# A router whose dense gate blocks are built earlier and stored in parts: stages swapped, picks moved up, sums of every third batch moved to VectorE

## The chip, the cores and the metric

The kernel runs on one core of a Trainium2 chip. The time is device time in microseconds (us) of one execution, as the median of several runs; lower is better. The engines are PE (TensorE), DVE (VectorE), ACT (ScalarE), POOL (GpSimd) and SP (SyncE), and 16 DMA engines move data between HBM and the on-chip memory. POOL issues the gathers here, SP most other transfers.

## What is computed

One layer of a decoder: attention branches, and then a channel mixer (PEER) with 16384 experts. Only the mixer matters here; it takes more than half of the time.

```
q = (hx @ w_pq).reshape(PEER_BLOCK, PEER_HEADS, 2, PK_HALF)
s = jnp.einsum('nhpc,hpkc->nhpk', q, sub_keys)
top_s, top_i = lax.top_k(s, PEER_TOPK)
cand = top_s[:, :, 0, :, None] + top_s[:, :, 1, None, :]
best_s, best = lax.top_k(cand.reshape(...), PEER_TOPK)
eidx = i1 * N_KEYS + i2
g = jax.nn.softmax(best_s, axis=-1)
a = jax.nn.gelu(jnp.einsum('nd,nhkd->nhk', hx, expert_u[eidx])) * g
return jnp.einsum('nhk,nhkd->nd', a, expert_v[eidx])
```

There are 1032 tokens (1024 and 8), 1024 features, 8 heads with two sets of 128 keys, and the 16 best pairs of each head: 128 experts for each token.

## The kernel before

Tokens are worked in tiles of 128. Tiles 0 to 4 and the tail of 8 tokens are **sparse**: their experts' rows are gathered. Tiles 5, 6 and 7 are **dense**: all 128 blocks of 128 experts are multiplied with them, and a gate matrix, zero for experts that a token has not picked, selects.

**Batches.** A sparse batch B gathers two experts for each token of a tile: two indirect DMAs of 128 rows of 8 KB (u and v of an expert side by side), 2.1 MB in all. B counts through the whole stage. Batches 0 to 33 are what is left of tile 0, batches 34 to 97 are tile 1, and batches from 98 on are tiles 2, 3, 4 and the tail. For each batch POOL gathers into `rows` (L2371); DVE makes the two dot products (L2460); ACT makes gelu and weight (L2542, L2545) and, before batch 98, two diagonal matrices of the weights (L2554), with which PE sums the rows into bank A (L2771). From batch 98 on DVE does the sums (`sums`, L2426). All engines walk through the same list of batches in order, and each has its further work written out at given batches.

**Sums on DVE.** `ON_VEC` lists batches whose rows DVE sums into `acc[0]` (`early_sums`, L2411) instead of PE. PE adds that partial sum once, in the last batch of the tile, with a multiplication by the identity (L2766).

**The ring.** `rows` has five places of one batch each. From `FEW_AT` to `MANY_AT` only places 0 to 2 are used (`place`): places 3 and 4 are then `second`, a store room for gate blocks. A gather waits until the batch that had its place before has been summed: `psum` counts the batches that PE has summed, `early` the sums of DVE.

**Batches 0 to 50: scores.** For each of 16 head halves (`hp`), three batches long (`LATE_PER`; called a triple here), PE makes queries (L2719) and scores (L2668), ACT copies them, and DVE takes the best 16 (`top16`, L2291 to L2298).

**Picks.** `PIECES` says in which batch DVE does which of five pieces for a tile: 0 and 2 are the best pairs of one half of the heads (`best_pairs`, L2096 to L2110), 1 and 3 the expert numbers (`indices`, L2119 to L2129), 4 the gates (`finish`). Piece 0 needs the top 16 of `hp` 0 to 7 alone. For a dense tile PE then turns the picks (`turn_picks`, L2732), and ACT copies them.

**Hots.** From batch `HOT0` on, three quads of four tokens in each of 32 batches: DVE (and partly ACT) writes one-hot rows (L2486, L2493), PE multiplies them to gates (L2743), and ACT copies the result into a stage (L2635). Sixteen quads make a gate block of 4 MB, which SP stores to `gates_dram` (L2317). There are six blocks and two stages, used in turn: the space `room` and the places `second`.

**Dense blocks.** SP loads u and v of one expert block (L2324, L2340) into four slots each of `room`, and the gates of two blocks (L2337). PE computes scores (L2782) and output (L2796), ACT gelu, DVE the product with the gates (L2501). In PE's order all this stands behind the sums of batch 97; the other engines go on with batches from 98 on, two expert blocks for every three batches.

Of the kernel before, what the change touches and what calls it, by code (L numbers as in the profile page):

```python
# [31 lines left out]
GBLK = 64  # L32
# [2130 lines left out]
def stage_ffn(c):  # L2163
# [23 lines left out]
    PICK0, HOT0, HOTS = HP * LATE_PER + 3, HP * LATE_PER + 10, 3  # L2187
# [7 lines left out]
    PIECES |= {PICK0 + at + step * k: (t, k) for t, at, step in zip(DENSE, (0, 6, 16), (1, 2, 2)) for k in range(5)}  # L2195
    PIECES |= {PICK0 + 29 + 3 * k: (2, k) for k in range(5)}
# [4 lines left out]
    ON_VEC = list(range(LATE_PER, first[1] - 1, LATE_PER))  # L2201
# [12 lines left out]
    FEW, FEW_AT, MANY_AT = 3, HOT0 - 2, HOT0 + QUADS // HOTS + 6  # L2214
# [6 lines left out]
    with ExitStack() as ctx:  # L2221
# [26 lines left out]
        stage = [t.rearrange("p (a n) -> p a n", n=GBLK) for t in (part(0, NK * GBLK), second)]  # L2248
# [16 lines left out]
        h_out = [c.sem(f"ff_h_out{i}") for i in range(2)]  # L2265
        g_in, g_out = ([c.sem(f"ff_{t}{i}") for i in range(2)] for t in ("g_in", "g_out"))
# [34 lines left out]
        with nc.Block() as block:  # L2301
            @block.sync
            def _(sp):
# [11 lines left out]
                for k in range(QUADS // BQ):  # L2315
# [12 lines left out]
                for e in range(NK):  # L2328
                    if e + 2 < NK:
                        load_u(e + 2)  # L2330
                    if e % 2 == 0:
                        f = e // 2
                        if f >= 2:
                            sp.wait_ge(s["d_a"], e - 2)
                        for half in range(2):
                            src = gates[half * GB:(half + 1) * GB, :, e:e + 2].rearrange("b p a n -> p b a n")
                            sp.dma_start(g2[f % 2][:, half], src).then_inc(g_in[f % 2], 16)  # L2337
                    if e >= 4:
# [13 lines left out]
            def _(pool):  # L2352
                for B, (i, b) in enumerate(batches):
# [5 lines left out]
                    if B == MANY_AT:  # L2359
                        pool.wait_ge(g_out[1], 16 * (QUADS // BQ // 2))  # L2360
# [30 lines left out]
            def _(dve):  # L2391
# [122 lines left out]
            def _(act):  # L2514
# [74 lines left out]
                for B, (i, b) in enumerate(batches):  # L2589
# [69 lines left out]
            def _(pe):  # L2659
# [87 lines left out]
                for B, (i, b) in enumerate(batches[0:BP]):  # L2747
# [10 lines left out]
                    if B not in ON_VEC:  # L2758
# [4 lines left out]
                        if B + 1 == first[1]:  # L2763
# [245 lines left out]
```

## Time and profile before

| | |
|---|---|
| median of 3 runs | 4294.34 us (4293.23 to 4304.6) |
| the profiled execution | 4304.18 us, span 4302.4 us |
| busy in the span | PE 87%, DVE 65%, ACT 30%, POOL 21% |
| mean granted clock of PE | 0.913 |
| moved by DMA | 1034.11 MB, 240 GB/s over the span |

Busy time is an average over stages with different limits, so the stages are to be read one by one. A granted clock of 1.0 is 2.4 GHz, and 0.5 is 1.2 GHz. The span begins with the first instruction; the mixer's batches begin at 1974 us in it.

### The profile page before, as it was taken

What the parts mean: (1) busy time and instruction counts of PE and PEld (TensorE: products, weight loads), DVE (VectorE), ACT (ScalarE), POOL (GpSimd) and SP (SyncE); (2) the same over time, 40 slices, a digit from 0 to 9 for tenths busy, and PEclk for the clock granted to TensorE, in tenths of its full rate; (3) what the DMA queues carried; (4) which work ended last, traced back from release to release, by engine and by line L of the source; (5) the groups of instructions that cost most, each with busy time, mean ns of one, the idle gap of its engine ahead of it and who ended that gap; (6) DMA issues with size and microseconds to landing.
All of it is one profiled execution on the core that took longest, in us unless ns stands there. A gap on an engine that the chain in (4) does not pass through costs nothing.

```text
span 4302.4 us, 43216 instructions
## 1 busy us (share of the span) xinstructions
PE 3735.0 (87%) x14282; PEld 2465.9 (57%) x14282; DVE 2813.1 (65%) x6473; ACT 1282.9 (30%) x3304; POOL 888.3 (21%) x714
## 2 busy tenths in 40 slices
PE   8898899999992798996999577689999999899896
PEld 6575377888881687884455255444544444454443
DVE  2764562442434348875996899756779776967966
ACT  2564442322322232542222267511111111111111
POOL 0000000001000001431232122233333333343332
PEclk9898998896895799997999788899999999999997
DMA  4001112213115444876887577899999999999997
GB/s 160 7 1 42 28 40 70 74 38 116 51 38 192 151 142 153 330 284 250 316 320 275 219 271 309 308 404 412 415 388 381 413 412 383 385 404 414 381 360 278
DMA packets 264044, 1034.11 MB, mean 240 GB/s; under 512 B 29547, under 2 KB 106755, under 8 KB 178707
## 3 DMA queue, kind: packets, MB, share of 16 engines
q0 software_dynamic: 101056, 721.50, 42.9%
q1 hardware_dynamic: 139874, 300.09, 19.0%
q10 hardware_dynamic: 22896, 9.80, 0.8%
q8 instruction: 115, 1.88, 0.2%
q14 instruction: 103, 0.84, 0.1%
HBM read 982.05 MB, written 49.25 MB: 240 GB/s over the span
## 4 chain that ended last, share of the span: by engine, by line
PE 23%; DVE 15%; DMA 13%; issue 2%; ACT 1%; SPq 0%; POOL 0%; DVEq 0%; ACTq 0%; POOLq 0%
DMA ff_room<-in_v 9%; PE banks L2796 8%; PE banks L2782 8%; DVE ff_rows L2460 4%; PE banks L2771 3%; PE banks L2719 3%; DVE mx_x L2486 2%; DMA ff_rows<-in_uv,pk_expert 2%; DMA mx_x<-gates_dram 1%; DVE region L2426 1%; DVE pk_eq L2124 1%; DVE o_mla_tops L2129 1%; DVE mx_x L2493 1%; DVE ff_acc L2426 1%; DVE pk_besti L2110 1%
## 5 line engine op out<-in xcount | busy, mean ns | idle before, releaser
L2796 PE MATMUL banks<-ff_room,mx_x 128*128 128x512 f32 x1536 | 702.0, 608 | 62.7 <-DMA ff_room<-in_v 31.9
L2460 DVE CUSTOM_DVE_ANT_0 ff_rows<-ff_rows,ff_h_row 128x1024 f32<-128x1024 f32 x588 | 696.5, 1221 | 86.9 <-DMA ff_rows<-in_uv,pk_expert 61.0
L2782 PE MATMUL banks<-mx_x,ff_room 128*128 128x384 f32 x2048 | 683.9, 487 | 11.2 <-ACT mx_x L2643 11.2
L2371 POOL DMA_INDIRECT ff_rows<-in_uv,region x324 | 418.6, 1292 | 808.6 <-DVE region L2426 540.9
L2782 PEld LDWEIGHTS banks<-mx_x,ff_room 128*128 128x128 f32 x2048 | 389.4, 190 | 311.3 <-issue 74.7
L2796 PEld LDWEIGHTS banks<-ff_room,mx_x 128*128 128x128 f32 x1536 | 296.8, 195 | 424.3 <-issue 355.8
L2371 POOL DMA_INDIRECT ff_rows<-in_uv,pk_expert x256 | 314.2, 1227 | 754.0 <-PE banks L2771 414.6
L2771 PE MATMUL banks<-ff_rows,o_mla_tops 128*128 128x512 f32 x704 | 356.7, 655 | 95.1 <-ACT o_mla_tops L2554 95.1
L2426 DVE SCALAR_TENSOR_TENSOR region<-ff_rows,ff_a,region 128x1024 f32<-128x1024 f32 x254 | 326.5, 1286 | 4.7
L2542 ACT ACTIVATE ff_gelu<-ff_dots 128x2 f32<-128x2 f32 x294 | 59.5, 203 | 846.0 <-DVE ff_dots L2460 845.8
L2771 PEld LDWEIGHTS banks<-ff_rows,o_mla_tops 128*128 128x128 f32 x704 | 142.2, 210 | 270.7 <-issue 152.6
L180 PE MATMUL banks<-d_w_high,h_high 128*128 128x512 f32 (+1 forms) x648 | 274.4, 423 | 21.9 <-DVE d_w_low L187 21.0
L2501 DVE TENSOR_TENSOR mx_x<-mx_x 128x384 f32<-128x384 f32 x128 | 71.3, 557 | 303.2 <-DMA mx_x<-gates_dram 177.1
L181 PE MATMUL banks<-d_w_low,h_high 128*128 128x512 f32 (+1 forms) x648 | 264.6, 408 | 0.0
L182 PE MATMUL banks<-d_w_high,h_low 128*128 128x512 f32 (+1 forms) x648 | 264.0, 407 | 0.0
L2643 ACT ACTIVATE mx_x<-banks 128x384 f32<-128x384 f32 x128 | 62.7, 490 | 623.4 <-PE banks L2782 623.4
L757 DVE TENSOR_TENSOR banks<-banks,region 128x128 f32<-128x128 f32 (+1 forms) x160 | 53.6, 335 | 256.8 <-PE banks L668 240.0
L1719 POOL DMA_INDIRECT mx_rows<-in_uv,region x60 | 100.8, 1681 | 508.7 <-DVE region L2146 342.9
L180 PEld LDWEIGHTS banks<-d_w_high,h_high 128*128 128x128 f32 (+1 forms) x648 | 166.4, 257 | 46.7 <-DVE d_w_low L187 10.4
L182 PEld LDWEIGHTS banks<-d_w_high,h_low 128*128 128x128 f32 (+1 forms) x648 | 166.7, 257 | 20.5
L181 PEld LDWEIGHTS banks<-d_w_low,h_high 128*128 128x128 f32 (+1 forms) x648 | 167.7, 259 | 18.2
L2719 PE MATMUL banks<-mx_x,ff_room 128*128 128x388 f32 x512 | 175.1, 493 | 0.0
(463 smaller groups left out, 6299.4 us busy)
## 6 DMA issues: line engine op xcount, KB each, us to landing
ff_room<-in_uT SPq DMA_DIRECT2D x128, 512.0 KB, 14.6
ff_room<-in_v SPq DMA_DIRECT2D x128, 512.0 KB, 20.8
mx_x<-gates_dram SPq DMA_DIRECT2D x128, 192.0 KB, 17.3
d_w<-in_w_dil POOLq DMA_DIRECT2D x9, 2048.0 KB, 8.4
d_w<-in_w_ada POOLq DMA_DIRECT2D x32, 512.0 KB, 5.0
mx_w<-in_w_gate SPq DMA_DIRECT2D x24, 512.0 KB, 5.5
gates_dram<-ff_room SPq DMA_DIRECT2D x3, 4096.0 KB, 14.6
gates_dram<-ff_rows SPq DMA_DIRECT2D x3, 4096.0 KB, 15.9
```

The source lines that it names most:

```text
L180: pe.matmul(out, w[0], x[0], start=start, stop=False)
L181: pe.matmul(out, w[0], x[1], start=False, stop=False)
L182: return pe.matmul(out, w[1], x[0], start=False, stop=stop)
L1719: pool.indirect_dma_start(out=ring[:, r, :], out_offset=None, in_=IN["uv"][:, :], in_offset=bass.IndirectOffsetOnAxis(ap=at, axis=0))\
L2371: pool.indirect_dma_start(out=rows[r][:, :], out_offset=None, in_=IN["uv"][:, :], in_offset=bass.IndirectOffsetOnAxis(ap=at, axis=0))\
L2426: ins = dve.scalar_tensor_tensor(out=y[:], in0=v, scalar=weight, in1=y[:], op0=ALU.mult, op1=ALU.add)
L2460: ins = dve.tensor_tensor_reduce(rows[r][:, 0:D], rows[r][:, 0:D], h_row[i % 2][:], 1.0, 0.0, ALU.mult, ALU.add, dots[:, place[B], j:j + 1])
L2486: ins = dve.tensor_scalar(hot1[q % RQ][:, k], c.iota[:], pick(0, at), pick(2, at), ALU.is_equal, ALU.mult)
L2719: ins = pe.matmul(Q[:, i, 0:CL], w[n % 2][:, k, :], c.h2[:, k, NE + i * CL:NE + (i + 1) * CL], start=(k == 0), stop=(k == KD - 1))
L2771: ins = pe.matmul(A[:, half], diag[:, n % DB, j], rows[r][:, D + half * 512:D + (half + 1) * 512], **ends)
L2782: ins = pe.matmul(SD[:, 0:ND], u[e % 4][:, k, :], hd[:, k, :], start=(k == 0), stop=(k == KD - 1))
L2796: ins = pe.matmul(Y[j][:, half], ad[e % 2][:, j * P:(j + 1) * P], v[e % 4][:, half_rows[half]], start=(e == 0), stop=(e == NK - 1))
```

## The change

- `ON_VEC` gets five batches of tile 1: 36, 39, 42, 45 and 48. Their rows are summed by DVE into `acc[1]`, the first of them with a plain product, and PE adds `acc[1]` in batch 97.
- Pieces 0 and 1 of dense tile 5 move from batches 51 and 52 to 36 and 40 (`HALF0`), and pieces 2 to 4 from 53, 54, 55 to 51, 52, 53. The pieces of tiles 6, 7 and 2 and the hots move up by two batches: `HOT0` is 56 and was 58, `FEW_AT` 54 and was 56.
- The two stages are swapped: blocks 0, 2 and 4 lie in `second`, and 1, 3 and 5 in `room`. So `second` is free after block 4, and `MANY_AT` is 88 and was 96.
- Block 5 is stored in eight parts of 0.5 MB, each with a semaphore of its own; a part lies where one slot of u or v will be. The first load into a slot waits for its part alone, and the loads of gates wait for the part that holds their columns.

```diff
-    PICK0, HOT0, HOTS = HP * LATE_PER + 3, HP * LATE_PER + 10, 3
+    PICK0, HOT0, HOTS = HP * LATE_PER + 3, HP * LATE_PER + 8, 3
+    HALF0 = HP // 2 * LATE_PER + 12
...
-    PIECES |= {PICK0 + at + step * k: (t, k) for t, at, step in zip(DENSE, (0, 6, 16), (1, 2, 2)) for k in range(5)}
-    PIECES |= {PICK0 + 29 + 3 * k: (2, k) for k in range(5)}
+    PIECES |= {HALF0 + 4 * k: (DENSE[0], k) for k in range(2)}
+    PIECES |= {PICK0 + k - 2: (DENSE[0], k) for k in range(2, 5)}
+    PIECES |= {PICK0 + at + 2 * k: (t, k) for t, at in zip(DENSE[1:], (4, 14)) for k in range(5)}
+    PIECES |= {PICK0 + 27 + 3 * k: (2, k) for k in range(5)}
...
-    ON_VEC = list(range(LATE_PER, first[1] - 1, LATE_PER))
+    ON_VEC = list(range(LATE_PER, first[1] - 1, LATE_PER)) + list(range(first[1] + 2, HP * LATE_PER + 1, LATE_PER))
...
-    FEW, FEW_AT, MANY_AT = 3, HOT0 - 2, HOT0 + QUADS // HOTS + 6
+    FEW, FEW_AT, MANY_AT = 3, HOT0 - 2, HOT0 + (QUADS - BQ) // HOTS + 6
...
-        stage = [t.rearrange("p (a n) -> p a n", n=GBLK) for t in (part(0, NK * GBLK), second)]
+        stage = [t.rearrange("p (a n) -> p a n", n=GBLK) for t in (second, part(0, NK * GBLK))]
...
-                for k in range(QUADS // BQ):
+                KL = QUADS // BQ - 1
+                for k in range(KL):
                     sp.wait_ge(s["hot_copy"], (k + 1) * BQ)
...
-                for k in range(2):
-                    sp.wait_ge(g_out[k], 16 * (QUADS // BQ // 2))
+                sp.wait_ge(s["hot_copy"], QUADS)
+                for i in range(8):
+                    cut = slice(i * NK // 8, (i + 1) * NK // 8)
+                    sp.dma_start(gates[KL, :, cut], stage[KL % 2][:, cut]).then_inc(g_part[i], 16)
+                sp.wait_ge(g_out[0], 16 * ((KL + 1) // 2))
+                sp.wait_ge(g_out[1], 16 * (KL // 2))
...
-                    if e >= 4:
+                    if e < 4:
+                        sp.wait_ge(g_part[e], 16)
+                    else:
                         sp.wait_ge(s["s_mm"], e - 3)
...
-                        pool.wait_ge(g_out[1], 16 * (QUADS // BQ // 2))
+                        pool.wait_ge(g_out[0], 16 * (QUADS // BQ // 2))
...
+                    fresh = i and B - LATE_PER not in ON_VEC
+                    if fresh:
+                        dve.wait_ge(h_out[0], 32)
...
-                        if B + 1 == first[1]:
-                            pe.wait_ge(s["early"], len(ON_VEC) * G)
+                        if B + 1 == first[i + 1]:
+                            pe.wait_ge(s["early"], by_vec(B) * G)
                             for half in range(2):
-                                pe.matmul(A[:, half], c.ident[:, :], acc[0][:, half_rows[half]], start=False, stop=False)
+                                pe.matmul(A[:, half], c.ident[:, :], acc[i][:, half_rows[half]], start=False, stop=False)
```

ACT waits before its first copy into a stage: for the sums of batches up to 53 ahead of the first copy into `second`, and for the last top 16 ahead of the first copy into `room`.

PE, batches 35 to 38 before the change (the sums of a batch are the rows with `ff_rows`, queries have `ff_room` and 128x388, scores 128x128):

```order
L2771 MATMUL banks<-ff_rows,o_mla_tops 128x512 x4
L2719 MATMUL banks<-mx_x,ff_room 128x388 x6
L2771 MATMUL banks<-ff_rows,o_mla_tops 128x512 x4
L2719 MATMUL banks<-mx_x,ff_room 128x388 x6
L2771 MATMUL banks<-ff_rows,o_mla_tops 128x512 x4
L2719 MATMUL banks<-mx_x,ff_room 128x388 x4
L2668 MATMUL banks<-ff_room 128x128 x6
```

The same place in the changed kernel, where L2719 is L2744, L2771 is L2796 and L2668 is L2693:

```order
L2796 MATMUL banks<-ff_rows,o_mla_tops 128x512 x4
L2744 MATMUL banks<-mx_x,ff_room 128x388 x12
L2796 MATMUL banks<-ff_rows,o_mla_tops 128x512 x4
L2744 MATMUL banks<-mx_x,ff_room 128x388 x4
L2693 MATMUL banks<-ff_room 128x128 x6
L2693 MATMUL banks<-ff_room 8x128
```

The four sums of batch 36 have gone, and two groups of queries stand next to each other; so it is in batches 39, 42, 45 and 48.

DVE, batches 36 and 37 before (a dot product is an `ISA` row with `ff_h_row` and the row behind it):

```order
L2291 MAX o_mla_tops<-ff_room 128x8 x6
L2291 MAX o_mla_tops<-ff_room 8x8
L2460 ISA ff_rows,ff_dots<-ff_rows,ff_h_row 128x1024
L2460 ISA ff_dots 128x1
L2460 ISA ff_rows,ff_dots<-ff_rows,ff_h_row 128x1024
L2460 ISA ff_dots 128x1
L2293 MAX_INDEX topi<-o_mla_tops,ff_room 128x8
L2294 MATCH_REPLACE ff_room<-o_mla_tops,ff_room 128x128
L2293 MAX_INDEX topi<-o_mla_tops,ff_room 128x8
L2294 MATCH_REPLACE ff_room<-o_mla_tops,ff_room 128x128
```

DVE in batch 36 of the changed kernel, from the first step of the top 16 on, where L2291 is L2295:

```order
L2295 MAX o_mla_tops<-ff_room 128x8 x6
L2295 MAX o_mla_tops<-ff_room 8x8
L2096 TENSOR_TENSOR pk_cand<-o_mla_tops 128x1024
L2100 MAX pk_best<-pk_cand 128x8 x4
L2103 MAX_INDEX pk_besti<-pk_best,pk_cand 128x8
L2104 MATCH_REPLACE pk_cand_rest<-pk_best,pk_cand 128x256
```

The best pairs of tile 5 now stand between the first step of the top 16 and the dots of batch 37. Behind the second dot of batch 37 the changed kernel has:

```order
L2484 ISA ff_rows,ff_dots<-ff_rows,ff_h_row 128x1024
L2484 ISA ff_dots 128x1
L2432 TENSOR_SCALAR ff_acc<-ff_rows,ff_a 128x1024
L2434 SCALAR_TENSOR_TENSOR ff_acc<-ff_rows,ff_a,ff_acc 128x1024
L2297 MAX_INDEX topi<-o_mla_tops,ff_room 128x8
L2298 MATCH_REPLACE ff_room<-o_mla_tops,ff_room 128x128
```

The two sums of batch 36 (`ff_acc`) have come in ahead of the second step of the top 16.

SP, from the stores of the gate blocks on, before:

```order
L2317 DMA gates_dram<-ff_room 128x8192
L2317 DMA gates_dram<-ff_rows 128x8192
L2317 DMA gates_dram<-ff_room 128x8192
L2317 DMA gates_dram<-ff_rows 128x8192
L2317 DMA gates_dram<-ff_room 128x8192
L2317 DMA gates_dram<-ff_rows 128x8192
L2324 DMA ff_room<-in_uT 128x1024 x3
L2337 DMA mx_x<-gates_dram 128x3x128 x2
L2340 DMA ff_room<-in_v 128x1024
```

And in the changed kernel, where L2317 is L2322, L2324 is L2336, L2337 is L2350 and L2340 is L2355:

```order
L2322 DMA gates_dram<-ff_rows 128x8192
L2322 DMA gates_dram<-ff_room 128x8192
L2322 DMA gates_dram<-ff_rows 128x8192
L2322 DMA gates_dram<-ff_room 128x8192
L2322 DMA gates_dram<-ff_rows 128x8192
L2327 DMA gates_dram<-ff_room 128x1024 x8
L2336 DMA ff_room<-in_uT 128x1024 x3
L2350 DMA mx_x<-gates_dram 128x3x128 x2
L2355 DMA ff_room<-in_v 128x1024
```

The blocks begin in `ff_rows` (`second`) instead of `ff_room`, and the last has become eight stores of 128x1024 that stand ahead of the first load of u.

## Rows read from the trace of the kernel before

**Rows 1.** Windows by stage: stretch, length, busy PE, PEld, DVE, ACT, POOL, clock, DMA, GB/s.
```profile
2060.00:2252.00 192.00, 177.76 (x559) 95.14 (x558) 186.08 (x708) 51.29 (x168) 57.80 (x53) 0.99 0.85 319
2252.00:2374.00 122.00, 114.78 (x348) 59.64 (x347) 78.33 (x344) 30.36 (x105) 36.42 (x35) 1.00 0.76 285
2374.00:2431.00 57.00, 32.73 (x55) 12.76 (x53) 46.36 (x115) 11.75 (x36) 8.36 (x9) 0.76 0.42 160
2431.00:2760.00 329.00, 244.66 (x1027) 159.60 (x1028) 312.26 (x985) 219.18 (x508) 73.84 (x68) 0.85 0.75 287
2760.00:2825.00 65.00, 38.92 (x85) 18.00 (x85) 23.21 (x43) 18.24 (x49) 19.71 (x18) 0.82 0.90 356
2825.00:4242.00 1417.00, 1339.24 (x3575) 682.32 (x3574) 1075.44 (x1567) 196.30 (x707) 522.16 (x390) 0.98 1.00 397
```

**Rows 2.** Timeline of PE in batches 36 to 39: start, length, what.
```profile
2267.18 4.07 PE L2719 MATMUL banks<-mx_x,ff_room 128*128 128x388 f32 x12
2271.09 3.60 PE L2771 MATMUL banks<-ff_rows,o_mla_tops 128*128 128x512 f32 x8
2274.52 4.07 PE L2719 MATMUL banks<-mx_x,ff_room 128*128 128x388 f32 x12
...
2291.05 4.07 PE L2719 MATMUL banks<-mx_x,ff_room 128*128 128x388 f32 x12
```

**Rows 3.** Timeline of DVE: the wait in batch 36, and the start of batch 51.
```profile
2264.85 1.44 DVE L2291 MAX8 o_mla_tops<-ff_room 128x8 f32<-128x128 f32 x7 [9.96 <-ACT ff_room L2535]
...
2373.58 1.23 DVE L2460 CUSTOM_DVE_ANT_0 ff_rows<-ff_rows,ff_h_row 128x1024 f32<-128x1024 f32 x1
```

**Rows 4.** Timeline of DVE: the starts of batches 27 and 30.
```profile
2197.18 1.23 DVE L2460 CUSTOM_DVE_ANT_0 ff_rows<-ff_rows,ff_h_row 128x1024 f32<-128x1024 f32 x1
...
2215.26 1.23 DVE L2460 CUSTOM_DVE_ANT_0 ff_rows<-ff_rows,ff_h_row 128x1024 f32<-128x1024 f32 x1
```

**Rows 5.** Timeline of DVE: batches 52 (two rows), 53, 55 and 56.
```profile
2385.01 1.22 DVE L2460 CUSTOM_DVE_ANT_0 ff_rows<-ff_rows,ff_h_row 128x1024 f32<-128x1024 f32 x1
...
2387.30 0.19 DVE L2119 TENSOR_SCALAR pk_part<-pk_besti 128x64 uint32<-128x64 uint32 x1
...
2394.50 1.23 DVE L2460 CUSTOM_DVE_ANT_0 ff_rows<-ff_rows,ff_h_row 128x1024 f32<-128x1024 f32 x1
...
2415.84 1.22 DVE L2460 CUSTOM_DVE_ANT_0 ff_rows<-ff_rows,ff_h_row 128x1024 f32<-128x1024 f32 x1
...
2419.01 1.22 DVE L2460 CUSTOM_DVE_ANT_0 ff_rows<-ff_rows,ff_h_row 128x1024 f32<-128x1024 f32 x1
```

**Rows 6.** Timeline of POOL: the first gather of batch 57.
```profile
2425.42 0.94 POOL L2371 DMA_INDIRECT ff_rows<-in_uv,pk_expert  x1 [26.50 <-PE banks L2771]
```

**Rows 7.** Timeline of DVE: the starts of batches 58, 60 and 90.
```profile
2444.97 1.22 DVE L2460 CUSTOM_DVE_ANT_0 ff_rows<-ff_rows,ff_h_row 128x1024 f32<-128x1024 f32 x1
...
2465.26 1.22 DVE L2460 CUSTOM_DVE_ANT_0 ff_rows<-ff_rows,ff_h_row 128x1024 f32<-128x1024 f32 x1
...
2760.46 1.22 DVE L2460 CUSTOM_DVE_ANT_0 ff_rows<-ff_rows,ff_h_row 128x1024 f32<-128x1024 f32 x1
```

**Rows 8.** Timeline at the dense start: POOL batch 92, SP, DVE batch 97, PE.
```profile
2755.27 0.94 POOL L2371 DMA_INDIRECT ff_rows<-in_uv,pk_expert  x1 [3.52 <-PE banks L2771]
...
2769.07 0.32 SPq L2317 DMA_DIRECT2D gates_dram<-ff_rows  x1
...
2782.75 1.28 SPq L2324 DMA_DIRECT2D ff_room<-in_uT  x3
...
2818.80 1.23 DVE L2460 CUSTOM_DVE_ANT_0 ff_rows<-ff_rows,ff_h_row 128x1024 f32<-128x1024 f32 x1 [2.15 <-DMA ff_rows<-in_uv,pk_expert]
...
2825.10 5.32 PE L2782 MATMUL banks<-mx_x,ff_room 128*128 128x384 f32 x16
```

**Rows 9.** Timeline of PE: partial sum added in batch 33; sums of batch 54.
```profile
2245.50 1.88 PE L2766 MATMUL banks<-region,ident 128*128 128x512 f32 x4
...
2409.83 5.86 PE L2771 MATMUL banks<-ff_rows,o_mla_tops 128*128 128x512 f32 x8 [4.97 <-ACT o_mla_tops L2554]
```

More of the change, by code:

```diff
@@ L2265, in stage_ffn @@
         h_out = [c.sem(f"ff_h_out{i}") for i in range(2)]
+        g_part = [c.sem(f"ff_g_part{i}") for i in range(8)]
         g_in, g_out = ([c.sem(f"ff_{t}{i}") for i in range(2)] for t in ("g_in", "g_out"))
@@ L2334, in _ @@
                             sp.wait_ge(s["d_a"], e - 2)
+                        sp.wait_ge(g_part[e * 8 // NK], 16)
                         for half in range(2):
@@ L2337, in _ @@
                             sp.dma_start(g2[f % 2][:, half], src).then_inc(g_in[f % 2], 16)
-                    if e >= 4:
+                    if e < 4:
+                        sp.wait_ge(g_part[4 + e], 16)
+                    else:
                         sp.wait_ge(s["y_mm"], e - 3)
@@ L2404, in early_sums @@
                 def early_sums(B):
+                    i = batches[B][0]
+                    y = acc[i]
                     dve.wait_ge(s["a"], B + 1)
+                    fresh = i and B - LATE_PER not in ON_VEC
+                    if fresh:
+                        dve.wait_ge(h_out[0], 32)
                     for j in range(G):
@@ L2410, in early_sums @@
                             dve.wait_ge(s["early"], n)
-                        dve.scalar_tensor_tensor(out=acc[0][:], in0=v, scalar=weight, in1=acc[0][:],
-                                                 op0=ALU.mult, op1=ALU.add).then_inc(s["early"], 1)
+                        if fresh and j == 0:
+                            ins = dve.tensor_scalar(y[:], v, weight, None, ALU.mult)
+                        else:
+                            ins = dve.scalar_tensor_tensor(out=y[:], in0=v, scalar=weight, in1=y[:], op0=ALU.mult,
+                                                           op1=ALU.add)
+                        ins.then_inc(s["early"], 1)
                 def sums(B):
@@ L2627, in _ @@
                             if q == 0:
+                                act.wait_ge(s["psum"], by_pe(FEW_AT - 1))
+                                act.wait_ge(s["early"], len(ON_VEC) * G)
+                            elif q == BQ:
                                 act.wait_ge(s["top"], 4 * HP)
-                            elif q == BQ:
-                                act.wait_ge(s["psum"], by_pe(FEW_AT - 1))
                             else:
```

## The prediction

> **What bounds the kernel now.** I read the busy time by stage first [rows 1]. From 2825 us on, the dense stage, the DMA engines are busy all the time (share 1.00, 397 GB/s): it ends when its bytes are moved, and the change leaves those bytes alone. Ahead of it they are not full: 0.85, 0.76, 0.42, 0.75 and 0.90 in five stretches. So the end moves with the moment at which the dense stage begins, that is, with PE's first dense matmul behind batch 97, at 2825.10 [rows 8]. What holds it up differs by stretch.
>
> In batches 36 to 50 (2252 to 2374 us) PE is busy for 114.8 of 122 us and DVE for 78.3: PE is the bound. The timeline of PE shows why: a triple of batches takes 23.87 us (2267.18 to 2291.05), and the sums of one batch 3.43 of that (2271.09 to 2274.52) [rows 2]. DVE waits for the scores ahead of each triple, 9.96 us in batch 36 [rows 3].
>
> From 2374 to 2431 both PE (32.7 of 57 us) and DMA (0.42) are mostly idle. DVE works through the picks of tile 5, which nothing else can go around, and then the ring shrinks from five places to three: POOL waits 26.50 us before it may gather batch 57 [rows 6], since that place was batch 55's, and batch 55's dots come behind four long pieces. So DVE stands still behind them, too.
>
> From 2431 to 2760, the hots, DVE is busy for 312.3 of 329 us: the bound is DVE [rows 1]. From 2760 on gathers, the last gate block and the first u and v fill the DMA engines to 0.90.
>
> **The change, part by part.** Times are those of the profiled execution.
>
> *Sums of five batches to DVE.* A PE triple shrinks to 23.87 - 3.43 = 20.44 us. DVE does such triples, sums included, in 18.08 us where PE lets it, as the batches 27 to 30 show (2197.18 to 2215.26) [rows 4]. So DVE could follow.
>
> *Pieces 0 and 1 of tile 5 to batches 36 and 40.* A dot pair takes 2.29 us (2385.01 to 2387.30); dots and best pairs 11.43 (batch 51 at 2373.58, batch 52 at 2385.01), so best pairs 9.14; the numbers 7.20 (2387.30 to 2394.50) [rows 3, 5]. The pieces stand behind DVE's wait for the scores, not inside it, so they don't just fill that idle time. Two chains have to be followed to batch 51, and the later one counts:
> - DVE alone, from the end of the top 16's first step in batch 36 (2264.85 + 1.44 = 2266.3): 9.1 + 7.2 for the pieces, four triples of 18.08, and batches 49 and 50, a triple less one dot pair and one such step (18.08 - 2.29 - 1.44 = 14.35). Batch 51 starts at 2369.3.
> - PE alone: four triples of 20.44 from 2267.18 end at 2348.9. Two waits come in, for the dots that stand behind the two pieces. Batch 37's dots end at 2266.3 + 9.1 + 2.3 = 2277.7, and PE, two query groups of 3.91 us after 2267.18, is ready for them at 2275.0. That is 2.7 us, and I take 4 with ACT's steps in between: 2357. DVE's step stands 2.3 us ahead of such a mark (2264.85 against 2267.18), so 2354.6 + 1.44 + 14.35 = 2370.4.
>
> Batch 51 thus starts at 2370.5 instead of 2373.58. That is little; but two of the five pieces are done by then, and five batches summed.
>
> *The rest of the picks and the shrinking ring.* From batch 51: dots and pairs 11.43, dots and numbers 9.49, dots and gates 3.17 (2415.84 to 2419.01), dots alone 2.29, dots and pairs of tile 6 11.43 [rows 5]; then hots begin, in batches 56 and 57, with what stood in 58 and 59: 20.29 (2444.97 to 2465.26) [rows 7]. Sum 58.1, and half a microsecond for the differences of the scores: batch 58 starts at 2429. Before, batch 60 stood at that point of the work at 2465.26. **36 us are won there**, if gathers keep up. They should: with three places from batch 54 on, batches 54 to 56 follow batches 50 to 52, all but the last long summed, and batch 57 follows 54, whose dots end at 2397.4. PE's sums there took 5.86 us at a lower clock [rows 9]; with some 2 us of ACT ahead of them and 10 for the gather behind (an estimate: 2.1 MB at 287 GB/s and the issue), its rows are there at 2415, as DVE comes to them (2415.8). What was a stall of 26 us becomes one of nothing to 5.
>
> *The hots* keep their work for each batch, and DVE is their bound, so they are moved whole: 295.2 us from batch 60 to batch 90 before [rows 7], from 58 to 88 now, to 2724.
>
> *Stages swapped, earlier five places.* Two batches more than before are left at that point, 90 to 97. Batch 92's gather, which before waited for the sums of batch 89, was issued at 2755.27 [rows 8]; now batch 90's stands there, at 2719, and 88 and 89 have gone ahead into the two places that block 4's store sets free. From 2719 the DMA engines have eight batches of 2.1 MB, block 5 (4.2 MB), four loads of u, two of v (0.52 MB each) and two of gates (0.2 MB) to move before the last of batch 97: 24.5 MB. At the 356 GB/s of that stretch before it takes 68.8 us, at the dense stage's 397 it takes 61.7 [rows 1]; I take the middle, 65, because gathers now wait in line earlier. From the last dot of batch 97 to the dense start took 6.3 us (2818.80 to 2825.10) [rows 8], and adding `acc[1]` costs PE 1.88 more [rows 9]. So 2719 + 65 + 6.3 + 1.9 = 2792: **33 us earlier** than 2825.1.
>
> *The store in eight parts.* Before, 13.7 us lay between the issue of block 5 and the first load of u (2769.07 to 2782.75) [rows 8]. A part can't land sooner than its eighth of that, 1.7 us, nor need it take longer than the whole did. Either way it costs the path nothing: PE may use u only behind batch 97, 42 us after that load before. The cover is the gathers; if they ended early, it would be worth up to 12 us. Seven more issues of 0.32 us lie on SP ahead of loads that have the same cover. ACT's waits for the swapped stages are for sums of batch 53 and a top 16 that are done when it comes to them; they cost nothing unless batch 53's sums are later than the first hot copy, some 12 us behind.
>
> Sum: 4304.18 - 33 = 4271 for the profiled execution. That one stands 9.8 us above the median of the runs shown, so for a median I say 4261.
>
> **Rivals.**
> - *Less* (a gain of 13 to 24 us). PE and DVE hold each other up in batches 36 to 50, so the pieces cost their full 16.3 us instead of the 8 that I gave to PE's waits, and batch 57's rows come 5 us late: 33 - 13 = 20, 4274. For it speaks that the pieces stand behind the wait; against it that PE, when it has caught up, needs 2.4 us more per triple than DVE, so DVE's delays are partly its own slack.
> - *More* (40 to 52 us). The DMA engines run at 397 GB/s from 2719 on, and DVE keeps to its own chain: 3.3 + 1.1, and up to 5 us of DVE's 17 idle in the hots: 43, 4251.
> - *No change.* The gathers, not DVE, carry the hots through three places, and what DVE saves ahead of them it waits for later. Against it: 329 us at 287 GB/s are 94 MB, which at 397 GB/s need 238 us; the engines have room for 90 us [rows 1]. The time would be 4294.
> - *Slower.* PE, which now stands waiting behind two pieces, falls to its lower level and stays there through batches 36 to 50. Eight matmul records of a sum take 3.60 us there now, and 5.86 in the stretch of mean clock 0.76 [rows 1, 2, 9]. A triple of 20.44 would be 33.3 us, four of them 51 us longer: 18 us slower than before, 4312. It decides from 8.3 us per triple on, a slowing by 1.4. Against it speaks the stretch from 2060 to 2252: there DVE is the bound too (busy 186.1 of 192), with the same pieces for tile 1, and the granted clock is 0.99 of 2.4 GHz [rows 1].
>
> The Trainium skill, "TensorE: Matmul & The Clock Gate", section "HAM oscillation — how this bites in real kernels", says that a tensor engine which waits inside every tile drops its clock in each wait and starts every tile cold. By that rule it is the slower case that comes. The trace agrees with it from 2374 to 2431, where waits go with a mean clock of 0.76, and not from 2060 to 2252.
>
> **How the numbers follow.** The forecast's own bounds are the two rates (a gain of 29 to 36) and 4 us for the chains to batch 51 and the ring: 24 to 40, so 4254 to 4270, with a chance of 0.62. Less: 0.12. More: 0.10. No change: 0.10. Slower: 0.06. The range of 4245 to 4282 takes in the first two and most of the third. This kernel's measurement tells some 0.3%, 13 us, from no change: faster by more than that 0.84, within it 0.10, slower 0.06.
>
> **What would show it.** In the changed profile: batch 51 starts at 2366 to 2376; DVE is busy for over 105 us from 2252 to 2374; no gather near batch 57 waits over 12 us; the hots' first one-hot row comes near 2413; PE's first dense matmul at 2785 to 2801, with the dense stage after it within 10 us of 1417. It is wrong if batch 51 is late by 10 us or more, if the granted clock there falls below 0.8, if DVE's busy share in the hots falls below 0.9, or if the dense stage starts early and grows longer.

## The result and the profile after

The changed kernel takes 4261.61 us, median of 4 runs (4260.13 to 4273.17), beside 4296.76 us for the kernel before on the same chip (4 runs): a ratio of 0.9912, 95% interval 0.9887 to 0.9937, so 35 us less. The profiled execution took 4273.17 us with a span of 4271.3 us (4302.4 before).

Windows by stage of the changed kernel, with the columns of [rows 1]. The first two stretches are those of [rows 1]; the others begin where the same work begins now, so the third overlaps the second by 3 us:

```profile
2060.00:2252.00 192.00, 178.27 (x556) 95.11 (x556) 185.41 (x700) 50.35 (x168) 56.90 (x52) 0.98 0.84 318
2252.00:2374.00 122.00, 106.02 (x312) 54.92 (x311) 107.30 (x405) 28.02 (x96) 35.25 (x33) 0.94 0.77 293
2371.00:2429.00 58.00, 38.12 (x92) 17.05 (x92) 56.90 (x159) 21.35 (x60) 14.59 (x13) 0.85 0.63 237
2429.00:2724.00 295.00, 225.65 (x970) 152.17 (x971) 277.95 (x887) 203.98 (x465) 63.20 (x59) 0.86 0.74 286
2724.00:2792.00 68.00, 49.33 (x108) 22.43 (x107) 33.01 (x68) 24.10 (x68) 26.03 (x24) 0.85 0.96 385
2792.00:4209.00 1417.00, 1335.88 (x3574) 681.51 (x3573) 1074.91 (x1566) 196.13 (x707) 522.09 (x389) 0.98 1.00 397
```

From 2252 to 2374 PE and DVE now share the work: 106.02 and 107.30 of 122 us, where it was 114.78 and 78.33 [rows 1]. In the next stretch DVE stands still for one of 58 us and DMA moves 237 instead of 160 GB/s. The hots are much as before, and ahead of the dense stage the DMA engines are nearly full: a share of 0.96 and 385 GB/s, where it was 0.90 and 356.

Timeline of the changed kernel in order of time (start, length, what, in brackets the wait ahead of it): the mixer's first gather (the same row of the kernel before stands at 1974.03), batches 36, 37 and 41, then the starts of batches 51, 58 and 88 (DVE), the gathers of 56, 57, 88 and 90 (POOL) and the first one-hot row (2413.67), SP from block 5 on, the last dot of batch 97 (2786.16), PE at the dense start:

```profile
1976.55 0.94 POOL L2386 DMA_INDIRECT ff_rows<-in_uv,region  x1 [42.42 <-POOLq L124]
2265.78 1.44 DVE L2295 MAX8 o_mla_tops<-ff_room 128x8 f32<-128x128 f32 x7 [9.96 <-ACT ff_room L2559]
2280.30 5.34 PE L2796 MATMUL banks<-ff_rows,o_mla_tops 128*128 128x512 f32 x8 [4.21 <-ACT o_mla_tops L2578]
2313.59 5.40 PE L2796 MATMUL banks<-ff_rows,o_mla_tops 128*128 128x512 f32 x8 [1.95 <-ACT o_mla_tops L2578]
2373.13 1.23 DVE L2484 CUSTOM_DVE_ANT_0 ff_rows<-ff_rows,ff_h_row 128x1024 f32<-128x1024 f32 x1
2395.92 1.73 POOL L2386 DMA_INDIRECT ff_rows<-in_uv,pk_expert  x1 [12.72 <-issue]
2407.81 0.93 POOL L2386 DMA_INDIRECT ff_rows<-in_uv,pk_expert  x1 [8.13 <-PE banks L2796]
2413.67 1.10 DVE L2510 TENSOR_SCALAR mx_x<-iota,mx_x 128x128 f32<-128x128 f32 x4
2431.67 1.22 DVE L2484 CUSTOM_DVE_ANT_0 ff_rows<-ff_rows,ff_h_row 128x1024 f32<-128x1024 f32 x1
2699.18 1.84 POOL L2386 DMA_INDIRECT ff_rows<-in_uv,pk_expert  x1 [5.82 <-DMA gates_dram<-ff_rows]
2726.16 0.94 POOL L2386 DMA_INDIRECT ff_rows<-in_uv,pk_expert  x1 [21.38 <-PE banks L2796]
2730.37 1.22 DVE L2484 CUSTOM_DVE_ANT_0 ff_rows<-ff_rows,ff_h_row 128x1024 f32<-128x1024 f32 x1
2738.84 4.22 SPq L2327 DMA_DIRECT2D gates_dram<-ff_room  x8
2747.38 7.71 SPq L2336 DMA_DIRECT2D ff_room<-in_uT  x3
2755.13 9.87 SPq L2350 DMA_DIRECT2D mx_x<-gates_dram  x2
2765.05 10.30 SPq L2355 DMA_DIRECT2D ff_room<-in_v  x1
2786.16 1.23 DVE L2484 CUSTOM_DVE_ANT_0 ff_rows<-ff_rows,ff_h_row 128x1024 f32<-128x1024 f32 x1 [2.25 <-DMA ff_rows<-in_uv,pk_expert]
2788.92 1.98 PE L2791 MATMUL banks<-ff_acc,ident 128*128 128x512 f32 x4 [1.81 <-ACT o_mla_tops L2578]
2794.18 5.32 PE L2807 MATMUL banks<-mx_x,ff_room 128*128 128x384 f32 x16
```

The dense stage begins at 2794.18 instead of 2825.10 [rows 8]. The part ahead of the mixer differs a little in every execution: the first gather of the mixer stands at 1974.0 us in the profile before and between 1969.8 and 1981.0 in the others. So from here on I count from that gather: 851.1 us to the dense start before, 817.7 after, and 2328.4 and 2294.8 us to the span's end. Both are 33 to 34 us shorter.

### The profile page after: what moved, and what is told of

Its sections match the earlier page's. It is cut to its first block, busy times and chain, and to the rows that moved or that the text cites. A ratio compares the mean times of both kernels' runs of the same rounds, so it can differ in the third digit from the quotient of the medians.

```text
span 4271.3 us, 43213 instructions
## 1 busy us (share of the span) xinstructions
PE 3723.5 (87%) x14246; PEld 2466.7 (58%) x14246; DVE 2825.4 (66%) x6483; ACT 1279.4 (30%) x3294; POOL 890.2 (21%) x714
## 4 chain that ended last, share of the span: by engine, by line
PE 22%; DVE 15%; DMA 13%; issue 2%; ACT 1%; POOL 0%; SPq 0%; DVEq 0%; ACTq 0%
DMA ff_room<-in_v 10%; PE banks L2821 8%; PE banks L2807 8%; DVE ff_rows L2484 4%; PE banks L2796 3%; PE banks L2744 2%; DVE mx_x L2510 2%; DMA ff_rows<-in_uv,pk_expert 1%; DVE region L2450 1%; DVE pk_eq L2124 1%; DVE o_mla_tops L2129 1%; DVE ff_acc L2450 1%; DVE mx_x L2517 1%; DVE pk_besti L2103 1%; DVE pk_besti L2110 1%
## 5 line engine op out<-in xcount | busy, mean ns | idle before, releaser
L2821 PEld LDWEIGHTS banks<-ff_room,mx_x 128*128 128x128 f32 x1536 | 295.2, 194 | 424.4 <-issue 355.0
L2796 PE MATMUL banks<-ff_rows,o_mla_tops 128*128 128x512 f32 x664 | 338.9, 659 | 74.0 <-ACT o_mla_tops L2578 74.0
L2796 PEld LDWEIGHTS banks<-ff_rows,o_mla_tops 128*128 128x128 f32 x664 | 134.3, 210 | 240.9 <-issue 147.4
L2668 ACT ACTIVATE mx_x<-banks 128x384 f32<-128x384 f32 x128 | 62.6, 489 | 597.7 <-PE banks L2807 597.7
L181 PEld LDWEIGHTS banks<-d_w_low,h_high 128*128 128x128 f32 (+1 forms) x648 | 167.7, 259 | 18.3
L2450 DVE SCALAR_TENSOR_TENSOR ff_acc<-ff_rows,ff_a,ff_acc 128x1024 f32<-128x1024 f32 x134 | 172.2, 1285 | 2.6
```

Of the source, the lines that this page charges most:

```text
L181: pe.matmul(out, w[0], x[1], start=False, stop=False)
L2450: ins = dve.scalar_tensor_tensor(out=y[:], in0=v, scalar=weight, in1=y[:], op0=ALU.mult, op1=ALU.add)
L2796: ins = pe.matmul(A[:, half], diag[:, n % DB, j], rows[r][:, D + half * 512:D + (half + 1) * 512], **ends)
L2821: ins = pe.matmul(Y[j][:, half], ad[e % 2][:, j * P:(j + 1) * P], v[e % 4][:, half_rows[half]], start=(e == 0), stop=(e == NK - 1))
```

## The experiments

Theory A is the prediction's: sums and earlier picks free time ahead of the hots, the earlier five places free some at their end, and the kernel ends as much earlier as PE's first dense matmul comes earlier. Theory F was formed on the way: what counts is how many bytes have been moved when the DMA engines have become full for good. The changed kernel was run beside each set of edits.

> The changed kernel itself, as the common measure for the runs beside it. Both theories: a median near 4262 us, 35 us under the kernel before, and PE's first dense matmul near 2794 us.

> The changed kernel as it is, as the measure for the runs beside it. Both theories: a ratio to the kernel before of 0.991 to 0.994; batch 51 starts 397 us and the first dense matmul 818 us behind the first gather, each within 2 us.

> The changed kernel as it is, as the measure for the runs beside it. All theories: a ratio of 0.991 to 0.994; 283.5 MB moved by the DMA engines in the 900 us behind the first gather.

4270.8, 4265.43 and 4261.64 us (ratios 0.9932, 0.9912, 0.9916; intervals 0.9911 to 0.9953, 0.9881 to 0.9942, 0.9884 to 0.9947). All profiles together, in us from the first gather; the last column is the rate over the first 900 us:

| kernel | batch 51 | dense start | end | GB/s |
|---|---|---|---|---|
| before | 399.6 | 851.1 | 2328.4 | 301 |
| changed (four profiles) | 396.3 to 397.5 | 816.3 to 818.7 | 2291.0 to 2294.8 | 315 to 316 |
| sums back on PE | 401.1 | 821.0 | 2298.7 | 313 |
| picks as before | 387.4 | 824.3 | 2306.6 | 309 |
| swap and parts alone | 399.2 | 836.5 | 2319.5 | 304 |
| stages as before | 397.3 | 828.0 | 2302.0 | 312 |
| one store | 396.7 | 817.4 | 2289.7 | 316 |
| order of places (both) | 396.2, 396.9 | 813.0, 813.1 | 2286.6, 2286.6 | 317, 317 |
| spread hots | 398.0 | 817.4 | 2299.8 | 312 |
| spread hots and places | 398.1 | 817.1 | 2286.5 | 317 |

The intervals of the ratios overlap in every comparison of an edit with the changed kernel beside it, so the medians alone prove none of the sizes below. These are read from the traces, one for each kernel. The four profiles of the changed kernel differ by 2.5 us at the dense start and by 3.8 us at the end; a difference under 4 us therefore tells nothing.

### Sums back on PE

```diff
-    ON_VEC = list(range(LATE_PER, first[1] - 1, LATE_PER)) + list(range(first[1] + 2, HP * LATE_PER + 1, LATE_PER))
+    ON_VEC = list(range(LATE_PER, first[1] - 1, LATE_PER))
```

The line by which PE adds `acc[1]` in batch 97 is left out with them.

> The changed kernel with the sums of batches 36, 39, 42, 45 and 48 given back to PE; all else stays. Theory A (the picks' move and the end of the stall at the ring carry the gain; the sums only make up for PE's waits behind the picks): PE's chain is four triples of 23.87 us from 2268 on, and with the sums of batch 36 between its queries PE comes to batch 37 at 2278, as its dots are ready, so the picks no longer cost PE anything. Batch 51 starts near 2375 instead of 2373, batch 97 saves 1.9 us of adding the partial sum, and the median is within 4 us of the changed kernel. Theory B (the sums carry a good part of the gain, five times 3.43 us): 17 us above the changed kernel, near 4279.

4277.67 us, ratio 0.995 (0.9925 to 0.9975): 7 us over the changed kernel's 4270.8, where theory A said at most 4 and theory B 17. Neither expectation was met. In the traces batch 51 is 4 to 5 us later and the end 4 to 8.

### Picks and hots as before

```diff
-    PICK0, HOT0, HOTS = HP * LATE_PER + 3, HP * LATE_PER + 8, 3
+    PICK0, HOT0, HOTS = HP * LATE_PER + 3, HP * LATE_PER + 10, 3
...
-    PIECES |= {HALF0 + 4 * k: (DENSE[0], k) for k in range(2)}
-    PIECES |= {PICK0 + k - 2: (DENSE[0], k) for k in range(2, 5)}
-    PIECES |= {PICK0 + at + 2 * k: (t, k) for t, at in zip(DENSE[1:], (4, 14)) for k in range(5)}
-    PIECES |= {PICK0 + 27 + 3 * k: (2, k) for k in range(5)}
+    PIECES |= {PICK0 + at + step * k: (t, k) for t, at, step in zip(DENSE, (0, 6, 16), (1, 2, 2)) for k in range(5)}
+    PIECES |= {PICK0 + 29 + 3 * k: (2, k) for k in range(5)}
```

> The changed kernel with all picks and the hots put back to the batches of before (hots from batch 58, three places from batch 56); sums on DVE, swapped stages and eight parts stay. Theory A: PE's triples of 20.44 us bring batch 51 to 2363, 10 us sooner than in either kernel, but the picks then stand in a row again and a gather near batch 57 waits over 20 us; batch 60 near 2455, dense start near 2805, median near 4275, 12 us above the changed kernel. Theory B: 17 us won by the sums, and the picks count for little: within 5 us of the changed kernel.

4282.83 us, ratio 0.9962 (0.994 to 0.9984): 12 us over 4270.8, as theory A said, and batch 57's gather waits as long as in the kernel before:

```profile
2415.88 0.94 POOL L2384 DMA_INDIRECT ff_rows<-in_uv,pk_expert  x1 [26.48 <-PE banks L2794]
```

PE's timeline in this kernel shows a triple with sums on DVE and no piece in it, from one start to the next:

```profile
2268.85 7.98 PE L2742 MATMUL banks<-mx_x,ff_room 128*128 128x388 f32 x24
...
2289.29 7.98 PE L2742 MATMUL banks<-mx_x,ff_room 128*128 128x388 f32 x24
```

That is 20.44 us, the number that the prediction worked out, and batch 51 stands at 387.4: 12 us ahead of the kernel before.

### Swap and parts alone

Both edits above at once; only the swapped stages, the parts and the earlier five places are left of the change.

> Only the swapped stages, the eight parts and five places from batch 90 on; picks, hots and sums as before. Theory A: up to batch 89 nothing moves, then gathers 93 and 94 go ahead into free places at 2758 instead of 2774 and the DMA engines are full from there: dense start near 2813, median 12 us under the kernel before, near 4285. Theory C (what the DMA engines can't do before 2770 they must do after it, and the part is worth nothing): as the kernel before, 4297.

4289.13 us, ratio 0.9981 (0.9951 to 1.001): 7 us below before, between theory A's 12 and theory C's 0, with an interval that reaches zero. In its profile the dense start is 14.6 us earlier than before and the end only 8.9. PE's waits in this kernel from 2810 to 2900 us (total, times, longest) show a wait for a load of v, which the kernel before does not have behind its dense start; the first row is this kernel's dense start:

```profile
2813.12 5.32 PE L2805 MATMUL banks<-mx_x,ff_room 128*128 128x384 f32 x16
PE banks L2819 <- DMA ff_room<-in_v: 11.3, 1, 11.3
```

These runs are two edits in all four combinations, with the swap in each. In the profiles, moving sums is worth 12.9 us without the picks (2319.5 to 2306.6) and 4 to 8 with them (from 2298.7 to between 2291.0 and 2294.8); moving picks 20.8 without the sums (2319.5 to 2298.7) and 12 to 16 with them. Together they are worth 25 to 28.5, not 34. At batch 51 it is the same: the sums bring it 11.8 us forward, the picks put it 1.9 us back, and both together bring it 1.7 to 2.9 us forward, not 9.9. The medians of the runs don't show this: 6.3 us for the sums, 11.5 for the picks (4289.13 to 4282.83 and to 4277.67) and 18.3 together, with a spread wider than the 5 to 9 us in question. My reading of the traces is that both edits draw on the idle time of DVE in batches 36 to 50. Windows of batches 36 to 50 of the kernel with sums on PE, columns as above:

```profile
2250.80:2372.90 122.10, 114.11 (x344) 58.99 (x343) 93.33 (x383) 30.39 (x105) 34.12 (x32) 1.00 0.77 282
```

and of the changed kernel:

```profile
2253.40:2373.10 119.70, 103.72 (x305) 53.68 (x305) 105.04 (x394) 27.22 (x95) 34.17 (x32) 0.94 0.78 298
```

With the sums PE is the bound, 114 of 122 us. Without them neither engine is: 104 and 105 of 120, and each stands idle for some 15 us, waiting for the other by way of ACT's copies.

### Stages as before

```diff
-    FEW, FEW_AT, MANY_AT = 3, HOT0 - 2, HOT0 + (QUADS - BQ) // HOTS + 6
+    FEW, FEW_AT, MANY_AT = 3, HOT0 - 2, HOT0 + QUADS // HOTS + 6
...
-        stage = [t.rearrange("p (a n) -> p a n", n=GBLK) for t in (second, part(0, NK * GBLK))]
+        stage = [t.rearrange("p (a n) -> p a n", n=GBLK) for t in (part(0, NK * GBLK), second)]
```

and block 5 in one store, with the waits that belong to it. Three things go back at once: the stages, the parts, and the five places (from batch 94 on, not 88).

> Sums and picks as in the changed kernel; the stages lie as before, block 5 is one store and five places come back at batch 94. Theory A (from the hots' end on, the bytes that are left set the end, and the earlier gathers by five places move some of them into time in which the DMA engines were not full): the first dense matmul comes 8 to 12 us later than in the changed kernel, 826 to 830 us behind the first gather, and the time is 7 to 12 us longer. Rival C (swap and parts only move transfers that the gathers hide anyway): within 3 us of the changed kernel.

4276.57 us, ratio 0.9931 (0.9906 to 0.9955), beside 4265.43: 11 us more, and the end is 11.0 us later than in the profile of the changed kernel beside it, the dense start 10.6. Beside all four profiles of the changed kernel the end is 7 to 11 us later. Theory A held, rival C fell. POOL's timeline in this kernel shows what the two missing places cost, at batches 91 and 95:

```profile
2735.47 0.94 POOL L2375 DMA_INDIRECT ff_rows<-in_uv,pk_expert  x1 [11.70 <-PE banks L2785]
...
2773.41 1.01 POOL L2375 DMA_INDIRECT ff_rows<-in_uv,pk_expert  x1 [22.98 <-PE banks L2785]
```

### One store for block 5

```diff
-                for i in range(8):
-                    cut = slice(i * NK // 8, (i + 1) * NK // 8)
-                    sp.dma_start(gates[KL, :, cut], stage[KL % 2][:, cut]).then_inc(g_part[i], 16)
+                sp.dma_start(gates[KL].rearrange("p a n -> p (a n)"), stage[KL % 2].rearrange("p a n -> p (a n)"))\
+                  .then_inc(g_part[0], 16)
```

> Block 5 is one store again and every first load waits for the whole of it; all else is the changed kernel. Theory A (the loads behind it have the gathers as cover): first dense matmul and time within 2 us of the changed kernel. Rival F (the end is set by the bytes that are moved once the DMA engines are full, so a transfer that starts later only changes the order): the time within 2 us as well, but the gathers, no longer behind the loads, land earlier and the dense stage begins 3 to 8 us earlier and is that much longer. Rival G (the parts matter): 5 to 12 us longer.

4261.47 us, ratio 0.992 (0.9894 to 0.9946), beside 4261.64, and the end stands at 2289.7, where the changed kernel's is at 2291.0 to 2294.8. The parts show no worth of their own; rival G fell. The earlier dense start that F expected did not come either (817.4).

### Order of places

```diff
-    place = [B % FEW if FEW_AT <= B < MANY_AT else (B - (0 if B < FEW_AT else first[TAIL])) % RB for B in range(len(batches))]
+    place = [B % FEW if FEW_AT <= B < MANY_AT else B % RB if B < FEW_AT else (3, 4, 1, 2, 0)[(B - MANY_AT) % RB] for B in range(len(batches))]
```

> The places from batch 88 on are used in the order 3, 4, 1, 2, 0, so that batch 90 takes over from batch 85 and 91 from 86, and none of them waits for the sums of batch 87, as 90 does in the changed kernel (21.4 us). Theory A (what was lost there is a gap of the DMA engines, whose share was 0.66 and 0.21 in the 20 us ahead of that gather): the first dense matmul comes 9 to 11 us earlier. Rival D (all five places are full at that time and wait for DVE, which works on hots without a pause until 2730 us, so an earlier gather of 90 only takes the turn of a later one): 2 to 4 us earlier.

> The order of places again, with more runs. Theory F (the time follows the bytes moved in the 900 us behind the first gather, 285.4 MB here and 283.5 in the changed kernel, at some 0.4 MB per us): 4 to 6 us faster than the changed kernel. Rival A (the first dense matmul sets the end): the same 4 to 6 us, since both moved together here. Rival H (chance): no difference.

4258.08 (0.9863; 0.9802 to 0.9924) and 4251.89 us (0.9902; 0.9867 to 0.9938), beside 4265.43 and 4261.64. Both medians are lower, by 7 and 10 us, but the intervals of the ratios overlap, so chance is not excluded by them. Part of it is the clock: among the runs with a mean clock of 0.915 to 0.917, the second set's four took 4248.69 to 4261.4 us, and the five of the changed kernel beside it 4256.66 to 4266.51, some 5 us apart. In the two traces the dense start is 3 to 6 us earlier and the end 4 to 8, both a little more than rival D's 2 to 4 and less than theory A's 9 to 11. The gap itself shows in a window of 10 us ahead of batch 90's gather of the changed kernel:

```profile
2716.20:2726.20 10.00, 6.53 (x16) 3.02 (x16) 9.73 (x18) 2.66 (x6) 0.04 (x1) 0.83 0.03 13
```

and at the same distance from the first gather with the new order:

```profile
2718.90:2728.90 10.00, 6.46 (x16) 3.06 (x16) 9.69 (x18) 2.66 (x6) 0.69 (x2) 0.83 0.99 411
```

The gap was filled, 0.99 for 0.03, and yet only about half of its 10 us came back: with five places full and DVE busy (9.7 of 10 us), batch 93 now waits 14.19 us for its place:

```profile
2744.72 1.50 POOL L2386 DMA_INDIRECT ff_rows<-in_uv,pk_expert  x1 [14.19 <-PE banks L2796]
```

That is rival D's mechanism.

### Spread hots

```diff
-        return range((B - HOT0) * HOTS, (B - HOT0 + 1) * HOTS) if HOT0 <= B < HOT0 + QUADS // HOTS else ()
+        n = B - HOT0
+        at = [8 * (m // 3) + 3 * (m % 3) for m in (n, n + 1)]
+        return range(*at) if 0 <= n < QUADS * 3 // 8 else ()
...
-    FEW, FEW_AT, MANY_AT = 3, HOT0 - 2, HOT0 + (QUADS - BQ) // HOTS + 6
+    FEW, FEW_AT, MANY_AT = 3, HOT0 - 2, HOT0 + (QUADS - BQ) * 3 // 8 + 6
```

> The same 96 quads of hots go over 36 batches, three, three and two in turn, instead of three in each of 32, and five places come back at batch 92. The work of DVE is the same. Theory A (behind the hots the DMA engines are full and DVE has nothing to do, while in the hots it is the other way round): four batches of 2.1 MB less are left behind the hots, which is 20 us at 415 GB/s, and the hots end four pairs of dots, 9 us, later: the first dense matmul comes 8 to 15 us earlier, and so does the end. Rival E (with three places the gathers of four more batches wait for sums each time): no gain, or up to 8 us later.

4278.33 us, ratio 0.9949 (0.9908 to 0.999), beside 4265.43: my expectation fell, and the time is rival E's. The waits for places that E named are there (14.81, 5.42, 9.38 and 11.70 us of POOL's in batches 88 to 91). But the dense start is where it was, and only the end is later, by 5 to 9 us. Block 5 was issued 779 us behind the first gather and not 762, the loads behind it are late, and the dense stage waits (PE, 2790 to 2900 us; 5.6 us in two waits there in the changed kernel). The dense start, block 5 and the wait:

```profile
2798.36 5.39 PE L2809 MATMUL banks<-mx_x,ff_room 128*128 128x384 f32 x16
2760.11 4.15 SPq L2329 DMA_DIRECT2D gates_dram<-ff_room  x8
PE banks L2823 <- DMA ff_room<-in_v: 11.9, 1, 11.9
```

With the order of places as well, and five places from batch 90 on:

```diff
-    FEW, FEW_AT, MANY_AT = 3, HOT0 - 2, HOT0 + (QUADS - BQ) * 3 // 8 + 6
+    FEW, FEW_AT, MANY_AT = 3, HOT0 - 2, HOT0 + (QUADS - BQ) * 3 // 8 + 4
...
+             (3, 4, 0, 1, 2, 3, 4)[B - MANY_AT] if B < MANY_AT + 7 else (2, 3, 0, 1, 4)[B % RB]
```

> Hots over 36 batches as before, but five places come back at batch 90 and not 92, and in an order in which each batch takes the place that comes free first. Theory F (bytes set the time; the spread hots lost by 3.8 MB less from 720 to 760 us behind the first gather than the order of places alone has, since their ring had three places for four batches longer): with the places back, 285 to 287 MB in 900 us and a time 4 to 9 us shorter than the changed kernel. Rival I (spreading the hots delays block 5 by 20 us, and with it the loads of u, v and gates, on which the dense stage then waits): slower than the changed kernel by 3 to 9 us, whatever the places.

4263.25 us, ratio 0.9925 (0.9896 to 0.9955), beside 4261.64. The trace went as F expected (317 GB/s, end at 2286.5), the median did not. Whether this version is faster than the changed kernel stays open; rival I's loss of 3 to 9 us shows in neither. Here PE is even ready ahead of the loads; its first dense matmul waits 13.74 us for one of u. Block 5 is as late as in the version above, 779 us behind the first gather, and the end is 13 us earlier all the same; so the late loads by themselves are not what the spread hots lost:

```profile
2749.59 4.94 SPq L2330 DMA_DIRECT2D gates_dram<-ff_room  x8
2787.39 7.09 PE L2810 MATMUL banks<-mx_x,ff_room 128*128 128x384 f32 x16 [13.74 <-DMA ff_room<-in_uT]
```

### What ties the end to the bytes

Windows from the first gather to 900 us behind it and from there to the end, of the kernel before:

```profile
1974.00:2874.00 900.00, 723.64 (x2409) 406.62 (x2408) 727.84 (x2397) 359.91 (x951) 237.95 (x218) 0.90 0.79 301
2874.00:4302.40 1428.40, 1316.89 (x3525) 672.69 (x3523) 1081.19 (x1593) 195.82 (x702) 510.85 (x381) 0.97 0.98 387
```

of the changed kernel:

```profile
1976.50:2876.50 900.00, 740.09 (x2449) 417.60 (x2448) 758.36 (x2431) 360.58 (x956) 248.49 (x226) 0.90 0.81 315
2876.50:4271.30 1394.80, 1283.79 (x3449) 656.80 (x3447) 1062.61 (x1569) 191.67 (x687) 502.35 (x373) 0.97 0.98 388
```

of the swap and parts alone:

```profile
1976.60:2876.60 900.00, 724.79 (x2414) 408.24 (x2413) 728.35 (x2398) 360.08 (x951) 241.59 (x220) 0.90 0.79 304
2876.60:4296.10 1419.50, 1315.27 (x3519) 672.70 (x3517) 1081.64 (x1591) 195.45 (x702) 507.48 (x379) 0.96 0.98 388
```

of the spread hots:

```profile
1981.00:2881.00 900.00, 728.38 (x2427) 410.20 (x2426) 756.23 (x2427) 359.46 (x952) 246.64 (x225) 0.90 0.81 312
2881.00:4280.80 1399.80, 1295.15 (x3471) 662.49 (x3469) 1066.42 (x1573) 192.68 (x691) 500.14 (x374) 0.97 0.98 388
```

and of the spread hots with places:

```profile
1970.30:2870.30 900.00, 735.21 (x2454) 413.77 (x2454) 761.18 (x2434) 360.69 (x956) 247.15 (x227) 0.91 0.82 317
2870.30:4256.80 1386.50, 1284.62 (x3443) 656.83 (x3441) 1060.81 (x1566) 191.48 (x687) 498.39 (x372) 0.97 0.98 389
```

All fourteen profiles move 823 to 825 MB behind the first gather (before: 0.9 x 301 + 1.4284 x 387 = 824), and behind the first 900 us all of them run at 387 to 389 GB/s. With 388 for all, the end is 900 + (824.2 - 0.9 x rate) / 0.388. This gives 2326 for the kernel before (2328.4), 2294 for the changed one (2294.8), 2319 for the swap and parts (2319.5), 2300.5 for the spread hots (2299.8), 2289 with places (2286.5), and it meets every one of the fourteen within 2.5 us. The dense start can't do that: the changed kernel and the two with spread hots begin it within 0.6 us of each other and end 13 us apart.

In part this is bookkeeping: where the bytes are the same and the rate behind 900 us is the same, the formula has to hold. What the traces show is that this rate is the same in all of them. That the DMA engines set it, and not PE, is argued and not tested, since no run changes the bytes of the dense stage alone. For it speaks that the DMA share there is 1.00 while PE is busy for 1336 of 1417 us; but PE's own busy time left behind 900 us, divided by a busy share of 0.924, meets the fourteen ends within 5.5 us, not far behind.

## Why the prediction was right

**The chains to batch 51** were right: forecast 2370.5 - 1974.0 = 396.5 us behind the first gather, measured 396.3 to 397.5. So was the reading that PE waits behind the pieces: 4.21 us ahead of batch 37's sums and 1.95 behind the second piece (at 2313.59). The prediction took 8 us for the two waits. They measured 6.2, but the eight matmul records behind each took 5.34 and 5.40 us, not 3.60, which the chain had put at nothing. Together that is 9.7 us, and the runs agree: sums alone bring batch 51 to 387.4, 12 us ahead of the kernel before (11 by the prediction's triples of 20.44), and the two pieces use up 9 to 10 of them.

**From 51 to 58**: 58.6 us forecast, 2431.67 - 2373.13 = 58.5 measured; the first one-hot row came at 2413.67 (2413 forecast). The stall of 26.50 us [rows 6] became 8.13 us of POOL's, where 0 to 5 was forecast, and DVE waits for none of it. One sign was missed by a little: batch 56's gather stands 12.72 us where I allowed 12, at no cost.

**The hots** were moved whole, and took 298.7 us (2431.67 to 2730.37) instead of 295.2. **The last gathers**: batch 90's was issued at 749.7 us behind the first gather, 745 forecast, late by the hots' 3.5 us and a little more. The term of 65 us measured 60.0 (2726.16 to 2786.16), which is what the upper of the two rates gave, 61.7; the last step of 6.3 + 1.9 measured 8.0. So two terms were off by 5 us each, in opposite directions. That the sum of 818 met 817.7 to a third of a microsecond is luck. In the range a bound was added up wrongly by one: 29 less 4 is 25, not 24.

**The parts** are covered, as I said, and show neither cost nor worth. But the seven more issues, put at 0.32 us each, were not so short: the eight took 4.22 us, and the loads of u, gates and v behind them 7.71, 9.87 and 10.30. **The swap** had no price of its own in the prediction; with the earlier places it is worth 7 to 11 us, a fifth to a third of the gain.

**The step that was wrong** is the rule that "the end moves with the moment at which the dense stage begins". It held here, where both moved by 33 us, and failed with the swap alone (14.6 us earlier, end 8.9) and the spread hots (no earlier, end 5 to 9 later). The end goes better with the bytes moved before the DMA engines are full for good: here 0.9 x 14 = 12.6 MB more in 900 us, which at 388 GB/s are 32 us.

**The slower rival** had its mechanism in the trace: PE waits inside batches 36 to 50, and the eight matmul records of the sum behind the wait take 5.34 us, not 3.60 [rows 2]. The granted clock of these 5.3 us was 0.68, between the two levels of 0.5 and 1.0, so PE was at the lower one for part of them:

```profile
2280.30:2285.60 5.30, 5.29 (x9) 2.38 (x10) 5.27 (x32) 0.00 (x0) 1.88 (x2) 0.68 0.55 184
```

But the mean clock of the whole stretch fell from 1.00 to 0.94 only, and PE was no longer the bound alone. On the Trainium skill's rule, "TensorE: Matmul & The Clock Gate", section "HAM oscillation — how this bites in real kernels" (each wait inside a tile makes the next one start cold), the trace agrees for the records behind such a wait, and not for the stage as a whole.

## What to carry to other kernels

When the last stage runs with full DMA engines, don't ask only when its first matmul starts, but also how many bytes have been moved by then: in these traces time was won where the DMA engines stood idle ahead of it, and an earlier or equal first matmul did not always mean an earlier end. Two edits on one stage need not add up: in the traces, which differ by up to 4 us among themselves, they gave 13 and 21 us alone and 25 to 28.5 together, though the medians of the runs can't tell this from a plain sum. And a gap filled in a ring of buffers can come back further on, as half of one did here, if the engine that empties the ring is busy without a pause.

## What was not expected of the hardware

- SP's issues were long behind the eight stores: two loads of gates took 9.87 us to issue and one of v 10.30 in the changed kernel. With block 5 as one store, so with seven transfers fewer ahead, the same rows take 0.97 and 3.23 us:

```profile
2751.39 0.97 SPq L2349 DMA_DIRECT2D mx_x<-gates_dram  x2
2752.41 3.23 SPq L2354 DMA_DIRECT2D ff_room<-in_v  x1
```

  That it is the number of transfers under way is a guess; a later load of v takes 8.03 us to issue in that kernel too. The time is the same.
- Within one kernel the runs spread with the granted clock: of the twelve runs of the changed kernel in the third set, the three with a mean clock of 0.923 or 0.924 took 4234.6 to 4240.0 us, and the four of 0.911 to 0.914 took 4272.5 to 4277.6. What sets the clock of a run, no run here shows. That spread, some 40 us, is as large as the change.
